# Router by pairwise ranks, a gather that reads normalised rows, and an expert buffer moved into the transposed rows, in a three-block transformer forward pass

## The reference

```python
mod = jax.nn.silu(c) @ w_ada[l] + b_ada[l]
sh1, sc1, ga1, sh2, sc2, ga2 = jnp.split(mod, N_MOD, axis=-1)
...
h2 = modulate(rms_norm(x, g_norm2[l]), sh2, sc2)       # h * (1 + scale) + shift
# hierarchical_moe(h2, ...):
g_logits = xt @ w_rg + b_rg                            # 4 groups
g_idx = jnp.argmax(g_logits, axis=-1)                  # the group's softmax weight is g_w
e_logits = (xt @ w_re + b_re).reshape(T, 4, 8)         # 8 experts in each group; those of g_idx
e_val, e_loc = lax.top_k(e_logits, 2)
e_w = jax.nn.softmax(e_val, axis=-1) * g_w
hid = jax.nn.silu(xb @ w1[e]) * (xb @ w3[e]);  ys = hid @ w2[e]     # for the chosen tokens xb of e
x = x + ga2 * (sum of ys * weight)
```

## Time and profile before

| | us |
|---|---|
| median of 3 runs (1417.03 to 1418.22) | 1417.8 |
| span of the profiled execution | 1419.6 |
| in it: up to the end of `W_O` | about 962 |
| from there to the first expert product | about 18 |
| from there to the end, 8 quads | about 439 |

### The profile page before, as it was taken

How to read it: one execution, slowest core, us unless ns; L and a number is a source line. 1 busy time by engine, 2 the same in 40 slices (tenths; PEclk the granted TensorE clock), 3 DMA queues, 4 the chain that set the end, 5 groups by cost and what they waited for, 6 DMA issues and landing times.

```text
span 1419.6 us, 15723 instructions
## 1 busy us (share of the span) xinstructions
PE 1229.2 (87%) x6651; PEld 807.1 (57%) x6651; DVE 651.7 (46%) x874; ACT 245.9 (17%) x501; POOL 59.9 (4%) x74
## 2 busy tenths in 40 slices
PE   8999999999999999999999999999564564655647
PEld 5889849994456776997445888655231221312212
DVE  6598426667855854567876764314110100101001
ACT  2332312220012421231002242013000000000000
POOL 1004100000000001000001200000000000000000
PEclk9999999999999999999999999999887887878878
DMA  9543335459953334546993443398999999999996
GB/s 348 161 149 129 119 133 178 164 179 333 350 205 119 119 119 149 178 177 219 348 351 125 166 149 126 124 428 321 428 428 428 428 427 428 428 428 428 428 424 255
DMA packets 94391, 376.96 MB, mean 266 GB/s; under 512 B 7248, under 2 KB 7920, under 8 KB 82416
## 3 DMA queue, kind: packets, MB, share of 16 engines
q1 hardware_dynamic: 93728, 373.84, 67.9%
q0 software_dynamic: 576, 2.10, 0.4%
q10 hardware_dynamic: 16, 0.00, 0.0%
HBM read 374.88 MB, written 1.05 MB: 265 GB/s over the span
## 4 chain that ended last, share of the span: by engine, by line
PE 74%; DMA 21%; DVE 2%; ACT 1%; issue 1%; POOL 0%; DVEq 0%; SPq 0%; ACTq 0%; POOLq 0%
PE PS L740 17%; PE PS L1016 14%; PE PS L969 12%; PE PS L787 9%; DMA weights<-in_w 8%; DMA arena<-in_w 7%; PE PS L1235 6%; DMA proj_rows<-in_w 4%; PE PS L723 4%; PE PS L1273 3%; DMA normalised<-in_w 2%; PE PS L679 2%; PE PS L1004 2%; PE PS L871 1%; PE PS L937 1%
## 5 line engine op out<-in xcount | busy, mean ns | idle before, releaser
L740 PE MATMUL PS<-weights,normalised 128*128 128x256 f32 x816 | 183.0, 380 | 2.1 <-DVE weights L1838 1.3
L1235 PE MATMUL PS<-weights,x_rows 128*32 128x512 f32 x368 | 132.0, 722 | 45.1 <-DMA proj_rows<-in_w 23.3
L740 PEld LDWEIGHTS PS<-weights,normalised 128*128 128x128 f32 x816 | 153.5, 190 | 26.5 <-issue 5.1
L1016 PE MATMUL PS<-weights,arena 128*128 128x512 f32 x384 | 167.4, 592 | 0.0
L2438 DVE TENSOR_TENSOR x_rows<-x_rows,PS 128x512 f32<-128x512 f32 x8 | 8.4, 1047 | 288.7 <-PE PS L1235 288.7
L1235 PE MATMUL PS<-arena,x_rows 128*32 128x512 f32 x256 | 94.0, 694 | 41.2 <-DMA weights<-in_w 28.7
L787 PE MATMUL PS<-weights,arena 128*128 128x512 f32 x288 | 125.0, 592 | 0.0
L1016 PEld LDWEIGHTS PS<-weights,arena 128*128 128x128 f32 x384 | 72.8, 190 | 90.9 <-issue 90.9
L1235 PE MATMUL PS<-proj_rows,x_rows 128*32 128x512 f32 x240 | 80.1, 716 | 46.3 <-DMA weights<-in_w 24.0
L969 PE MATMUL PS<-normalised,weights 128*128 128x128 f32 x896 | 106.9, 275 | 0.0
L969 PEld LDWEIGHTS PS<-normalised,weights 128*128 128x128 f32 x896 | 103.4, 192 | 0.0
(11 more groups left out here) (352 smaller groups left out, 1730.1 us busy)
## 6 DMA issues: line engine op xcount, KB each, us to landing
weights<-in_mlp_w SPq DMA_DIRECT2D x32, 2048.0 KB, 8.6
weights<-in_w SPq DMA_DIRECT2D x32, 2048.0 KB, 35.2
arena<-in_w SPq DMA_DIRECT2D x24, 2048.0 KB, 35.4
proj_rows<-in_w SPq DMA_DIRECT2D x16, 2048.0 KB, 34.4
weights<-in_ev_w_in SPq DMA_DIRECT2D x10, 2048.0 KB, 8.6
weights<-in_w_in SPq DMA_DIRECT2D x10, 2048.0 KB, 7.8
proj_rows<-in_w_ada SPq DMA_DIRECT2D x16, 1024.0 KB, 10.8
early_weights<-in_w SPq DMA_DIRECT2D x8, 2048.0 KB, 37.2
```

The lines of the kernel that those rows point to most:

```text
L740: last = mm(at, lhs[:, k, :], rhs[:, k, :], start=(first and k == 0), stop=(k == 3), skip_group_check=not first)
L1016: last = mm(PS[:, bank, :], lhs[:, k0 + i, rows], rhs[:, i, :], start=(g == 0 and i == 0), stop=(g == NGRP - 1 and i == 1))
L1235: last = mm(PS[CAP * x:CAP * (x + 1), 4 + kind, :], XG[:, k, CAP * x:CAP * (x + 1)], w[:, k, :], start=(k == 0), stop=(k == KT - 1), tile_ ...
```

## The change

1. `ranks` takes the place of `first_max`: all pairs of the 4 groups (then of the 8 experts) are subtracted, compared and summed to ranks; group and experts follow by comparison with 0.5 and 1.5. Loops over the two tiles become one instruction. What only the weights and the number of rounds need is moved behind `chosen` and behind the first gather.
2. `gather` reads `XN`, the rows scaled by rstd alone. `scaled_by_rows` writes them permuted for this norm (reading `X` with a stride of 8 floats). The transposes back, ScalarE's four copies and `H2R` go. Gain and shift are put in when the gathered rows are taken from PSUM: four 128x128 pieces each on ScalarE and VectorE in place of one 128x512 copy each, with a count for each piece.
3. Since the features are now permuted at `HT` too, the router's weights, b_ada's fourth and fifth part and g_norm2 are loaded in that order (two loads more), and `column_modulation(1)` reads `AC` as weights with a stride of 8 floats.
4. Slot 8 becomes `HT` and the 2048 floats behind it; block 10 waits for `router_raw`, the end of the router's products.

Core of the diff:

```diff
@@ expert slots and small loads
             if s == WSLOTS + 4:
-                return XH[:, 0:BW]
+                return XA[:, TT * D:TT * D + BW]
...
-            ld("router_in", WR[:, :, NG:NG + NE], A["w_re_2"][0].rearrange("(k p) n -> p k n", p=P))
+            ld("router_in", WR[:, :, NG:NG + NE], A["w_re_2"][0].rearrange("(p k) n -> p k n", p=P))
...
+            ld("by_rows_in", BC[:, 24:40].rearrange("p (a k) -> p a k", a=2),
+               A["b_ada_2"][0, 3 * D:5 * D].rearrange("(a p k) -> p a k", a=2, k=KT))
+            ld("by_rows_in", BC[:, 40:48], A["g_norm2_2"][0].rearrange("(p k) -> p k", k=KT))
@@ SyncE
-            sp.wait_ge(sem("h2_raw"), 4)
+            sp.wait_ge(sem("router_raw"), 1)
             expert_load(10)
@@ TensorE, column_modulation
-                for j in range(4):
-                    for n in range(4):
-                        last = mm(PS[:, 7, 4 * j + n:4 * j + n + 1], AC[:, j, n * P:(n + 1) * P], ONE[:, 0:1],
+                for i in range(2):
+                    sums = AC[:, 2 * i:2 * i + 2, :].rearrange("q a b -> q (a b)")
+                    by_k = sums.rearrange(("q (k p) -> q k p", "q (p k) -> q k p")[l], k=KT)
+                    for k in range(KT):
+                        last = mm(PS[:, 7, 8 * i + k:8 * i + k + 1], by_k[:, k, :], ONE[:, 0:1],
                                   start=True, stop=True)
@@ TensorE, entry of the MoE
-            quad(6, [HT[:, j, 0:P] for j in range(4)]).then_inc(sem("h2_raw"), 1)
-            quad(7, [HT[:, 4 + j, 0:P] for j in range(4)]).then_inc(sem("h2_raw"), 1)
-            for half in range(2):
-                pe.wait_ge(sem("h2_rows"), half + 1)
-                quad(6 + half, [HT[:, 4 * half + j, P:T] for j in range(4)]).then_inc(sem("h2_raw"), 1)
             pe.wait_ge(sem("x_new"), 15)
+            open_rows(1, (1,))
             pe.wait_ge(sem("router_taken"), 1)
-            open_rows(1)
+            open_rows(1, (0,))
             keep_warm(5, 1)
...
-            pe.wait_ge(sem("h2_rows"), 4)
...
-                        last = mm(PS[:, 6 + dt // 4, ...], H2R[:, tt, dt * P:(dt + 1) * P],
+                        last = mm(PS[:, 6 + dt // 4, ...], XN[:, tt, dt * P:(dt + 1) * P],
...
-                        if kind == 0 and k == KT // 2:
-                            pe.wait_ge(sem("ex_xg1"), n + 1)
+                        if kind == 0:
+                            pe.wait_ge(sem(("ex_xg0", "ex_xg1")[k // 4]), 4 * n + k % 4 + 1)
@@ ScalarE (the four copies to H2R go; the two Exp stand behind the first take_gather)
-                a(XG[:, 0:4, :], PS[:, 6, :].rearrange("p (k t) -> p k t", k=4), ACT.Copy).then_inc(sem("ex_xg0"), 1)
+                for k in range(4):
+                    a(XG[:, k, :], PS[:, 6, k * P:(k + 1) * P], ACT.Identity, bias=MC[:, 2, k:k + 1],
+                      scale=GM[:, 1, k:k + 1]).then_inc(sem("ex_xg0"), 1)
@@ VectorE
+            def scaled_by_rows(tt):
+                rstd()
+                rows = X[:, tt, :].rearrange("t (p k) -> t k p", k=KT)
+                for half in range(2):
+                    v.tensor_scalar(XN[:, tt, half * NB:(half + 1) * NB].rearrange("t (k p) -> t k p", k=4),
+                                    rows[:, 4 * half:4 * half + 4, :], ST[:, tt:tt + 1], None, ALU.mult)\
+                        .then_inc(sem("xn_ready"), 1)
...
+            def ranks(x, width, at):
+                other = x.unsqueeze(2).to_broadcast([P, TT, width, width])
+                own = x.unsqueeze(3).to_broadcast([P, TT, width, width])
+                ahead = CK[:, C_AHEAD:C_AHEAD + 64].rearrange("p (a b) -> p a b", a=8)[:, 0:width, 0:width]
+                by = st(at, TT, width, width)
+                link(v.tensor_tensor(by, other, own, ALU.subtract))
+                link(v.tensor_tensor(by, by, ahead.unsqueeze(1).to_broadcast([P, TT, width, width]), ALU.is_ge))
+                rank = st(at + TT * width * width, TT, width)
+                link(v.tensor_reduce(rank, by, AX.X, ALU.add))
+                return rank
...
+            link(v.tensor_scalar(hg, ranks(gl, NG, 16), 0.5, None, ALU.is_lt))
+            link(v.tensor_tensor(sel, el.rearrange("p t g e -> p t e g"),
+                                 hg.unsqueeze(2).to_broadcast([P, TT, EG, NG]), ALU.mult))
             link(v.tensor_reduce(le, sel, AX.X, ALU.add))
+            rank = ranks(le, EG, 192)
+            link(v.tensor_scalar(both, rank, 1.5, None, ALU.is_lt))
+            tell(v.tensor_tensor(table(SEL), of_group, by_expert(both), ALU.mult), "chosen", 1)
...
+            def take_gather(n):
+                dve.wait_ge(sem("ex_gather"), n * 2 + 2)
+                for k in range(4):
+                    v.tensor_scalar(XG[:, 4 + k, :], PS[:, 7, k * P:(k + 1) * P], GM[:, 1, 4 + k:5 + k],
+                                    MC[:, 2, 4 + k:5 + k], ALU.mult, ALU.add).then_inc(sem("ex_xg1"), 1)
```

More of the change, by code:

```diff
@@ L31 @@
 BIG = 1.0e30
+TINY = 1.2e-38
 EV_IN, EV_OUT = 10, 3
@@ L63 @@
 C_STEP = C_PLACE + 64
-C_KEEP = C_STEP + 8
+C_AHEAD = C_STEP + 8
+C_KEEP = C_AHEAD + 64
 M_LEV = 0
@@ L169, in shape_constants @@
     keep[:, C_STEP:C_STEP + T // CAP] = np.arange(T // CAP) * CAP + 0.5
+    e, o = np.arange(8)[:, None], np.arange(8)[None, :]
+    keep[:, C_AHEAD:C_AHEAD + 64] = np.where(o < e, 0.0, TINY).astype(np.float32).reshape(1, 64)
     mix = np.zeros((P, M_END), np.float32)
@@ L693, in keep_warm, with open_rows @@
                     mm(PS[:, bank, :], IDN, CK[:, 0:NB], start=True, stop=True)
-            def open_rows(tt):
-                for half in range(2):
+            def open_rows(tt, halves=(0, 1)):
+                for half in halves:
                     mm(PS[:, 2 * tt + half, :], IDN, X[:, tt, half * NB:(half + 1) * NB],
@@ L1268, in quad_of_experts @@
                     else:
-                        pe.wait_ge(sem(("ex_xg0", "ex_xg1")[half]), n + 2)
+                        pe.wait_ge(sem(("ex_xg0", "ex_xg1")[half]), 4 * n + 8)
                     for kk in range(4):
@@ L1699, in _ @@
             take_gather(0)
+            act.wait_ge(sem("r_rows"), 1)
+            a(ST[:, 80:88], ST[:, 72:80], ACT.Exp).then_inc(sem("r_exp"), 1)
+            act.wait_ge(sem("r_rows"), 2)
+            a(ST[:, 98:100], ST[:, 96:98], ACT.Exp).then_inc(sem("r_exp"), 1)
             with act.Fori(0, QUADS - 1) as i:
@@ L2108, in mlp_seam @@
                 else:
-                    for i in range(2):
-                        tell(v.scalar_tensor_tensor(GM[:, i, :], MC[:, 2 * i + 1, :], 1.0,
-                                                    GC[:, (R_G1, R_G2)[i]:(R_G1, R_G2)[i] + 8], ALU.add, ALU.mult),
+                    for i, g in enumerate((GC[:, R_G1:R_G1 + 8], BC[:, 40:48])):
+                        tell(v.scalar_tensor_tensor(GM[:, i, :], MC[:, 2 * i + 1, :], 1.0, g, ALU.add, ALU.mult),
                              "gm_ready", i + 1)
@@ L2380, in _ @@
+            le = st(128, TT, EG)
             link(v.tensor_reduce(le, sel, AX.X, ALU.add))
-            h1, h2 = st(256, TT, EG), st(320, TT, EG)
-            first_max(le, EG, ST[:, 66:68], h1)
-            link(v.scalar_tensor_tensor(le, h1, -BIG, le, ALU.mult, ALU.add))
-            first_max(le, EG, ST[:, 68:70], h2)
-            link(v.tensor_tensor(st(384, TT, EG), h1, h2, ALU.add))
-            for tt in range(TT):
-                link(v.tensor_tensor(SEL[:, tt, :].rearrange("p (g e) -> p g e", g=NG), colb(hg[:, tt, :], EG),
-                                     midb(st(384, TT, EG)[:, tt, :], NG), ALU.mult))
@@ L2389, in _, with by_expert, table @@
-            dve.sem_inc(sem("chosen"), 1)
+            h1, h2, both = st(144, TT, EG), st(160, TT, EG), st(176, TT, EG)
+            rank = ranks(le, EG, 192)
+            link(v.tensor_scalar(both, rank, 1.5, None, ALU.is_lt))
+            def by_expert(x):
+                return x.unsqueeze(2).to_broadcast([P, TT, NG, EG])
+            of_group = hg.unsqueeze(3).to_broadcast([P, TT, NG, EG])
+            def table(t):
+                return t.rearrange("p t (g e) -> p t g e", g=NG)
+            tell(v.tensor_tensor(table(SEL), of_group, by_expert(both), ALU.mult), "chosen", 1)
@@ L2421, in _ @@
             link(v.tensor_tensor(h1, h1, h2, ALU.add))
-            for tt in range(TT):
-                link(v.tensor_tensor(CWC[:, tt, :].rearrange("p (g e) -> p g e", g=NG), colb(hg[:, tt, :], EG),
-                                     midb(h1[:, tt, :], NG), ALU.mult))
+            link(v.tensor_tensor(table(CWC), of_group, by_expert(h1), ALU.mult))
             def weights(n, i):
@@ L2459, in _ @@
             weights(0, 0)
-            take_gather(0)
+            link(v.tensor_scalar(ST[:, 4:12], CK[:, C_STEP:C_STEP + T // CAP], ST[:, 0:1], None, ALU.is_lt))
+            link(v.tensor_reduce(ST[:, 1:2], ST[:, 4:12], AX.X, ALU.add))
+            link(v.tensor_copy(RNDS[:, :], ST[:, 1:2]))
+            dve.sem_inc(sem("rounds"), 1)
             with dve.Fori(0, QUADS - 1) as i:
```

56 lines of the change are left out of this document (18 added, 38 removed).

## The result

The changed kernel takes 1422.05 us in the median of 9 runs (1420.69 to 1426.1), the kernel before 1417.22 in 9 runs on the same chip (1416.72 to 1418.38). The ratio is 1.0034, with an interval of 1.0026 to 1.0043: some 4.8 us **slower**, where +1.45 was forecast with a range up to 1421.7. The time fell outside the range, on the side of rival B.

The account below looks back on a forecast made before the run. TensorE's chain was taken to bound the kernel up to the MoE's entry, DMA from `first_rows` on. -2.1 (entry) + 0.15 (scaling) + 2.9 (strided loads) + 0.5 (clock) = +1.45 on 1417.8 gave 1419.3 us, range 1414.8 to 1421.7.

Parts of the forecast that it names:

- rival B: Second MLP's seam: low clock lasts into the next projection, loads at their upper price; 1421.7, up to 1423; chance 0.11.
- the step named as the weakest: Second MLP's seam: column products' 32 strided weight loads add 2.9 us, at 0.7 ns a column.
- Rival A: Second MLP's seam: TensorE reads strided weights for free; 1415.9 us, between 1414.8 and 1417; chance 0.30.
- The clock behind them: Second MLP's seam: row modulation runs wholly at the low clock, 3.62 in place of 3.12, adding 0.5 us.
- The entry: MoE's entry: earlier `SEL` and places give 2.1 us; first expert product 16.6 us behind `W_O` in place of 18.6.
- rival C: MoE's entry: TensorE idles, the clock falls, gather and first products take back 2 us or more; 1421.3; chance 0.06.
- The permuted scaling: Ahead of the router: `scaled_rows(1)` reading with a stride of 8 floats costs 0.15 us.
- The slot: SP's queue: issuing block 10 at about 969.3 in place of 972.37 costed at nothing, since the queue drains anyway.
- 437 within 0.6: Expert stage: the stretch from SP's issue behind `first_rows` to the end stays unchanged at 437 us within 0.6.
- 3.4 and -1.95: Second seam: 2.9 for strided loads plus 0.5 for the clock; entry: -2.1 plus 0.15 for scaling.

Follow-up runs that it names:

- experiment 2: Kernel before, with only the second MLP's column products reading at a step of 8 floats, ScalarE permuting the sums first: 1423.93 us, ratio 1.0038.
- experiment 8: Kernel before, unchanged, profiled a second time: span 1416.3 us, that execution took 1418.12 us.
- experiment 5: Changed kernel with column products read contiguously and two warming products of 256 columns at the MoE's entry: 1416.34 us, ratio to before 0.9984.
- experiment 3: Changed kernel, with ScalarE putting the sums into the router's order so that TensorE loads them contiguously: 1416.44 us, ratio to before 0.999.
- experiment 6: Kernel before with `ranks` in place of `first_max`, transposes back and `H2R` kept: 1417.98 us, ratio 0.9995.
- experiment 4: Changed kernel with two warming products of 256 columns at the MoE's entry: 1420.65 us, ratio to before 1.002.
- experiment 7: Changed kernel with block 10 issued at `chosen` in place of `router_raw`: 1424.08 us, ratio 1.0034.
- experiment 9: Changed kernel with the old choice of experts (`first_max`) and its old order around `chosen`: 1424.75 us, ratio 1.0046.
- experiment 1: Small separate program without the model, timing TensorE weight loads and moving operands at several steps, and VectorE at stride 8: 0.108 us a load contiguous, 0.226 to 0.230 at 4 and 8.
- experiment 10: Experiment 5 with row modulation ahead of the column products in both MLP seams: 1418.43 us, ratio to before 0.9998.

## Why the prediction was wrong

**The column products, the step named as the weakest, failed by its size.** The mechanism was right (TensorE pays for a stride, on the chain, microsecond for microsecond), but the term of 2.9 us was taken from the middle of three prices on two other engines, 0.7 ns a column. It measured 3.9 (7.37 - 3.46, in experiment 2 as in the changed kernel), 0.95 ns a column, a little above the upper bound of 3.7 from ScalarE's copies. Rival A, which had 0.30, is refuted: a stride of 8 floats isn't free. A range over other engines was no substitute for the price on this one.

**The clock behind them was sized from too little.** I took 0.5 us, the difference between 3.12 and 3.62, as if 3.12 were what the seam always costs. The five profiles with contiguous column products differ in this. The clock falls in the seam in before, experiment 8 and experiment 5, which take 8.08, 7.77 and 8.04 us from the column products to the next projection; it doesn't in experiments 3 and 6, which take 6.40 each, with row modulation and four transposes at 1.82 + 0.45 = 2.27 us in place of the earlier trace rows's 3.97. The five with strided loads (after and experiments 2, 4, 7 and 9) take 12.02 to 12.44, and row modulation with transposes is at 4.0 to 4.4 each time. The means are 7.3 and 12.2: 4.9 us, of which 3.9 are the loads and 1.0 the clock, twice the 0.5. The times of experiment 2 say 5.4 (3.4 to 7.2) and would leave 1.5 for the clock; the profiles don't show where the other 0.5 would lie, and it is within the interval. Rival B priced the same mechanism, but put it into the next projection, and that part is wrong: the projection's first twelve passes are 5.39 in after as in its neighbours.

**The entry: every step up to the gather was right, and the last was missing.** `SEL` 3.21 us behind the addition (3.25 predicted); warming over 0.65 us before it; from the addition of the biases to the gather's start 975.88 - 970.92 = 4.96 us, against 976.45 - 969.25 = 7.20 before, so 2.2 gained (2.1 predicted). Then rival C happened, which the sum had put at nothing and the chances at 0.06: the granted clock fell, and the gather took 5.47 - 3.81 = 1.66 back. The argument against C was that the same small products had left the clock at 1.00 before; but before, they had followed on the warming product without a gap, and now 0.65 us of idle time stand ahead of them. That idle time was in the prediction (971.8 to 972.5); its price stood only in rival C. The amount of idle time alone doesn't decide: before, TensorE had idled for 0.69 and 0.22 us among the transposes back and for 0.50 ahead of the gather, 1.4 in all, and kept its clock; after, it was 0.65 and 0.40. What decides isn't shown, only that two products of 256 columns were enough. Experiments 4 and 5 show that nothing else is missing in the entry: with TensorE kept busy the entry is 16.5 us, where 16.6 was forecast.

**The small steps held.** The permuted scaling takes 0.65 a half (0.6 to 0.8 was the band in which at most 0.35 is lost); experiment 1 gives the stride's part as 0.20. The Trainium skill ("VectorE: DVE Perf Modes", Mode 2×_2P) doesn't ask for unit stride. The runs agree only in part: the strided `tensor_scalar` is faster than the contiguous two-source instruction (0.62 against 0.69 us), but it isn't at its own contiguous 0.43, as that rule alone would have it. The slot was worth nothing (experiment 7). From SP's restart to the end of the span it took 437.4 us before and 436.5 after; in all profiles of the study it is 436.1 to 437.7, where 437 within 0.6 was forecast.

**The sum by what was measured.** By the profiles it is 3.9 (loads) + 1.0 (clock behind them) - 0.53 (entry) = 4.4, by the time of experiment 2 it is 5.4 - 0.53 = 4.9; the ratio says 4.8, with 3.7 to 6.1. The forecast had 3.4 and -1.95. Of the error of some 3 us 1.0 are the loads, 0.5 to 1.0 the clock behind them and 1.4 the entry (1.66 for the clock in the gather, less 0.2 by which the steps ahead of it were better). So about two thirds of the miss are the granted clock in two places, and one third is the price of a strided load.

**The time of one execution was taken for the kernel's.** I set 1419.6 beside 1417.8 and passed over the difference, which was 3.6 us and not 1.8, since a span leaves out some 1.9 us of the time. A second profile of the same kernel spans 1416.3 (experiment 8). Of the 3.3 us between them 1.1 lie ahead of the first MLP's seam, 1.9 in it (416.55 to 426.05 against 415.49 to 423.06) and 0.3 in the second. The profile of after had no such excess (its execution took 1421.73, against the median of 1422.05), and this is why the two spans hide the loss.

What stays open: why the same code keeps its clock in one execution and loses it in another. The first MLP's seam, which no experiment but the tenth touched, shows column products of 3.46 to 4.49 us and row modulation of 1.82 to 3.62. With five profiles of either kind, the 1.0 us of clock in the second seam is a mean over few cases. The slow first passes at the start stand beside a granted clock of 1.00 (windows from 12 to 16 us, in both profiles); what slows them wasn't tried.

## What to carry to other kernels

A permutation costs something in the instruction that reads or writes it: put it where the engine has cover (here ScalarE, idle in that stretch), and not into a weight load on the path, which took about twice as long from a step of 4 floats on. When a change takes work away from TensorE ahead of something dense, ask for the granted clock that the rest will get; two short products of no other use kept 1.6 us of a gain of 2.2. A term for the clock needs a price in the sum, even where a similar stretch kept its clock. Two parts that each hide the other (transposes back, choice of experts) can give nothing one by one (the ranks alone 0, the gather alone a loss) and pay only together, so cost them as a pair. And take the base of each term from more than one execution, or from the one nearest to the median.

## What the runs showed of the hardware

- TensorE's weight load of 128x128 fp32: 0.108 us a pass at a step of 1 float, 0.114 at 2, 0.172 at 3, 0.226 at 4, 0.230 at 8, 0.210 at 16. At a step of 4 the record of one load has the same mean at a granted clock of 1.00 and of 0.50 (328 and 329 ns). Contiguous column products are not so: 3.46 us at 1.00, but 4.15 and 4.49 in seams where the clock falls during them (experiment 10, second seam; experiment 3, first seam). The moving operand, 128 columns: 0.111, 0.114, 0.227 and 0.233 us at steps of 1, 2, 4 and 8.
- VectorE, 512 fp32 with a step of 8 floats: `tensor_scalar` 427 to 624 ns reading and 633 writing, `tensor_tensor` 692 to 1081.
- The granted clock fell to 0.50 (1.2 of 2.4 GHz) in the gather when TensorE had idled for 0.65 us, run five small products and idled for 0.40 (after, experiments 3 and 7: gather 5.46 or 5.47); with 0.22 us idle and a product of 256 columns more on either side it stayed at 1.00 (experiments 4, 5 and 10: 3.72). After 2.50 us idle it was at 0.50 for the whole gather (experiment 9: 6.36). With no idle time between warming and small products, and 0.50 ahead of the gather, it stayed at 1.00 (before and experiment 6: 3.81).
- The same code at the second MLP's seam, with contiguous loads, kept its clock in two executions and lost it in three: 6.40 against 7.77 to 8.08 us.
- The first four passes of the first projection take 1.95 us in some profiles and up to 3.75 in others, with the same code.
